# Attention's gate and output blocks all ahead of z, and the last four blocks of the other gate moved in front of the delta rule's output projection

## The chip, the cores and the metric
The kernel runs on one NeuronCore of one Trainium2 chip. The metric is the device time of one execution in microseconds (us), the median of several runs. One program holds instruction streams for five engines: TensorE (PE, matmuls into the eight PSUM banks), VectorE (DVE), ScalarE (ACT), GpSimd (POOL) and SyncE (SP, which issues the DMAs). They meet only through semaphores.

## The reference, cut to what matters
Two transformer blocks in float32 on x of 256 tokens by 2048 features. The change is in the first block's mixer, which adds latent attention and a gated delta rule, each through its own output matrix and its own gate:

```
h = rmsnorm(x) * (1 + sc_a) + sh_a
p = h @ w_in                 # c_q, c_kv, k_pe, q_g, k_g, v_g, z, b, a, gate_logits
y_a = mla_branch(...) @ w_o_mla                   # attention
o   = gated_delta_chunked(q, k, v, beta, g)       # 8 heads of 128
o   = o * rsqrt(mean(o * o) + eps) * gdn_norm * silu(z)
y_b = o @ w_o_gdn
g_a, g_b = split(sigmoid(gate_logits))
x = x + gt_a * ((g_a * y_a + g_b * y_b) @ w_o)
```

Feed-forward layers and the whole second block follow and are not touched.

## The kernel before, in words
Activations lie feature-major, as [128 features, 256 tokens] for each of 16 slices. Each float32 value is kept as a high part and a low part in a reduced format, side by side: H1 holds h so (16 slices of 512 columns), H2 the inputs of the other projections. Weights come as 128x128 tiles, eight to a unit of 512 KB, in exactly the order in which the program uses them. For each unit ACT makes the high part (`hi`, L566, into HI), DVE the low part (`lo`, L722, into LO), and PE multiplies, adding hi·hi, hi·lo and lo·hi. A "wide" tile does this with two matmuls, one of 512 and one of 256 columns (L360 to L364), a narrow one with three of 256 (L366 to L368). There are five buffers for raw units (`NRAW`) and three each for HI and LO. Between the units of this region the same five buffers also take rows of the ada matrix, three for four units, which DVE reduces with one instruction each (`unit_dot`, L710). SP issues every load, in the order of the program, each when its buffer is free.

The order of all work is written by one Python walk, `walk`, that every engine's program replays. `block` emits the tiles of one output and hands its evacuation over with `later(generator, lag)`; `w.flush()`, called each second tile, takes one step of each pending generator that is due, usually three or four tiles (`LAG`, `EVLAG`) after its last step. `need(list, i)` looks at whether a result has been emitted; if not, `force()` takes a step of pending generators whether they are due or not. This orders instructions and is no wait on the chip by itself.

The stages around the change, with their tiles:
- the attention heads, pipelined beside the delta rule (`gdn`, a pending generator whose steps lie four tiles apart). Attention's eight outputs are split into H2[8..15].
- `gate_b(j)`, j from 0 to 15: a wide block of 16 tiles, H1 times w_in; its result is half of a sigmoid (sum, then tanh) in GB[j] (in the trace GBT). GB shares its memory with H2[0..7].
- `gate_a(j)`: a wide block of 16 tiles for YA[j], then a narrow block of 8 tiles over H2[8..15] with w_o_mla, attention's output; `ev_ya` multiplies it with the gate on DVE (L768).
- z: eight wide blocks of 16 tiles; sum, tanh and one multiplication each. Z lies in B1, over the delta rule's k and v of heads 0 to 3, so `need(hg_done, 0)` stands ahead of it.
- `onorm` and `gated(h)`: the delta rule's output is normed, multiplied with Z[h] (L764) and split by ACT (L577) and DVE (L760) into H2[8 + h], where attention's output was. For this `gated` does nothing until `mo_read[0]` is set: the count of the tile that reads attention's outputs last.
- the delta rule's projection w_o_gdn, narrow, 128 tiles over H2[8..15]: the first five outputs interleaved, then eleven one by one. `ev_yb` multiplies with GB[j] (L768), adds YA[j] (L764) and splits into H1[j] (L577, L758); this needs `h1_free`, the last tile that reads H1 for the gates. In its course x is loaded once more (`reload`, L323, four loads of 512 KB, due 24 tiles into the stage, waiting for `x_free`).
- w_o, 256 tiles, and the rest of the network.

Of the kernel before, what the change touches and what calls it, by code (L numbers as in the profile page):

```python
# [85 lines left out]
class Walk:  # L86
# [25 lines left out]
    def now(self):  # L112
        return [(s, n) for s, n in self.count.items() if s in SIGNALS]

    def later(self, gen, lag=0, gap=LAG):
        self.pending.append([self.tile + lag, gen, gap])
# [22 lines left out]
    def need(self, lst, i):  # L139
        while lst[i] is None:  # L140
            self.force()
        return lst[i]
# [26 lines left out]
def run(gen):  # L169
    for _ in gen:  # L170
        pass
# [30 lines left out]
def program(nc, xT, pos, cols_d, consts_d, wada, wst, bias_d, gain_d, out, log):  # L202
# [8 lines left out]
    with ctx:  # L211
# [96 lines left out]
        def sync(e):  # L308
# [35 lines left out]
            def store(m, a, ready):  # L344
                q.wait_ge(ready)
                e.dma_start(out[:, m, a:a + 1024], YT[:, m, a:a + 1024]).then_inc(S["out"], 16)

            walk(dict(load_cols=load_cols, load_consts=load_consts, load_x=load_x, load_x2=load_x2, load_pos=load_pos,
                      load_ada=load_ada, load_unit=load_unit, load_bias=load_bias, load_gain=load_gain, store=store), log)
            e.wait_ge(S["out"], 16 * N_STORES)  # L350

        def tensor(e):
# [184 lines left out]
            def conv_square_sum(bk, a, square, free):  # L537
                q.wait_ge(square, free)
                for j in range(a, a + 4):
                    r = e.matmul(bk[:, 0:256], cn("ones"), B1[:, j, :], start=(j == 0), stop=(j == 7))  # L540
                r.then_inc(S["cv_p"], 1)

            walk(dict(tile=tile, tile_tokens=tile_tokens, x_turn=x_turn, direct=direct, c_spread=c_spread, spin=spin, stat_add=stat_add, stat_sum=stat_sum, acc2_sum=acc2_sum, rope_turn=rope_turn, kpe_swap=kpe_swap, ba_turn=ba_turn,
                      cumulate=cumulate, row_sum=row_sum, spread=spread, g_spread=g_spread, g_heads=g_heads, g_turn=g_turn,
                      g_turn_mt=g_turn_mt, g_pair=g_pair, g_ws=g_ws, g_state=g_state, g_out=g_out, turn=turn,
# [3 lines left out]
        def scalar(e):  # L549
# [131 lines left out]
            def conv_tanh(y, t, ready, free):  # L681
                q.wait_ge(ready, free)
                e.activation(y, t, ACT.Tanh, scale=0.5).then_inc(S["cv_a"], 1)

            walk(dict(c_sigmoid=c_sigmoid, half_row=half_row, modulated=modulated, hi=hi, copy_sum=copy_sum, split_hi=split_hi, tanh=tanh, sigmoid=sigmoid, square=square,
                      gained=gained, square_sum=square_sum, root_table=root_table, root_guess=root_guess, sine=sine, beta=beta, softplus=softplus, gate_exp=gate_exp, row_square=row_square,
                      soft_exp=soft_exp, soft_scale=soft_scale, tap_first=tap_first, conv_first=conv_first, padded=padded, turned_rows=turned_rows, turned=turned, g_exp=g_exp, g_copy=g_copy, conv_square=conv_square, conv_affine=conv_affine, conv_tanh=conv_tanh))
# [297 lines left out]
        def walk(mine, log=None):  # L985
            w = Walk(mine)
# [135 lines left out]
            def block(H, toks, k0, wname, kbase, n, evac, order=None, wide=False):  # L1122
                return blocks(H, toks, k0, wname, kbase, [(n, evac)], order, wide)
# [348 lines left out]
            def l2norm(hg):  # L1472
                order = [(b + 4 * hg + i, n + i) for i in range(4) for b, n in ((8, 4), (0, 0))]
                while None in [qkv_tok[j] for j, n in order]:
                    yield
                bi, bk, fr = mbank.get()
                for c, (j, n) in enumerate(order):
                    i, t, ft = te.get()
                    a = do("row_square", "l2_a", t, B1[:, j, :], qkv_tok[j], ft)
                    yield  # L1480
                    m = do("row_sum", "l2_p", bk, n, t, c == 0, c == 7, a, fr)
                    te.release(i, m)
                yield
                need(H2_tok, 7)
                while rs_busy[0]:
                    yield
                rs_busy[0] = True
                r = yield from rsqrt_steps(RS[:, 0, :], RS[:, 1, :], bk[:, 0:256], 1.0, 1e-6, m, H2_tok[7], rs_used[0])
                mbank.release(bi, r)
                yield  # L1490
                for n in range(0, 8, 2):
                    bi, bk, fr = mbank.get()
                    m = do("spread", "l2_p", bk, n, r, fr)
                    rs_used[0] = m
                    yield
                    for i in range(2):
                        j = (0 if n < 4 else 8) + 4 * hg + n % 4 + i
                        qkv_tok[j] = do("unit_rows", "l2_v", bk, j, i, 128.0 ** -0.5 if n < 4 else 1.0, m)
                    mbank.release(bi, qkv_tok[j])
                l2_tok[hg] = qkv_tok[j]  # L1500
                rs_busy[0] = False
# [369 lines left out]
            mo_read = [None]  # L1871
# [14 lines left out]
            def ev_gate(dst, toks, j, free):  # L1886
                def f(bk, tok, own):
                    k = yield from raw_sum(dst[j], bk, tok, own, free)
                    yield
                    toks[j] = do("tanh", "ev_a", dst[j], dst[j], 0.5, k)  # L1890
                return f

            def ev_ya(j):
                def f(bk, tok, own):
                    ya_tok[j] = do("scaled", "ev_v", YA[j], YA[j], 1.0, bk[:, 0:256], add, mult, tok, need(ga_tok, j))
                    own[0].release(own[1], ya_tok[j])
                    yield
                return f

            def gate_a(j):  # L1900
                run(block(H1, h_tok, 0, "w_in", 0, 42 + j, ev_gate(YA, ga_tok, j, mla_free), wide=True))
                run(block(H2, mo_tok, 8, "w_o_mla", 0, j, ev_ya(j)))

            def gate_b(j):
                run(block(H1, h_tok, 0, "w_in", 0, 58 + j, ev_gate(GB, gb_tok, j, up_free), wide=True))
# [2 lines left out]
                ups(h)  # L1908
            up_free = ("tile", w.tile)
            later(l2norm(1), 0, 6)  # L1910
            for j in range(16):
                gate_b(j)
            need(mo_tok, 7)
            mla_free = now()
            for j in range(12):
                gate_a(j)
            need(hg_done, 0)
            for j in range(8):
                run(block(H1, h_tok, 0, "w_in", 0, 33 + j, ev_z(j), wide=True))
            for j in range(12, 16):  # L1920
                gate_a(j)
            h1_free = mo_read[0] = ("tile", w.tile)
            need(hg_done, 1)
            x_free = now()

# [633 lines left out]
```

## Time and profile before

| | us |
|---|---|
| median of 3 runs | 2774.64 (2770.35 to 2775.34) |
| the profiled execution's own time | 2774.21 |
| its span, first to last instruction | 2772.4 |
| mean granted TensorE clock | 0.992 |
| PE busy | 2697.3 (97%) |
| DVE busy | 1943.1 (70%) |
| ACT busy | 1308.3 (47%) |

Times in rows are microseconds from the start of the span, durations of single instructions nanoseconds where it says so. Consecutive matmuls overlap, so a matmul's own duration is longer than the distance to the next one; PE's pace is read from the starts. "idle before <-releaser" is how long the engine stood idle before an instruction and what ended that. The clock is a share of 2.4 GHz.

### The profile page before, as it was taken

Reading aid. Unit: us, or ns where it says so; the run is one execution under the profiler, and the core shown is the slowest. Engines: PE = TensorE matmul, PEld = TensorE weight load, DVE = VectorE, ACT = ScalarE, POOL = GpSimd, SP = SyncE. Lnnn points to the kernel's source line nnn. Section 1 sums busy time; section 2 is a strip of 40 time slices with the busy share of each in tenths; the row PEclk is TensorE's granted clock in tenths of the full one; section 3 lists DMA queues with packets and bytes.
Section 4 is the critical chain, followed back from the end, with each engine's and each line's share of the span. In section 5 each row is a group of like instructions: output and inputs, shape, how many; then the busy total and the mean of one; then the engine's idle time right before and its main releaser. Section 6 shows DMA issues by size and latency. Waiting matters only on the chain.

```text
span 2772.4 us, 41156 instructions
## 1 busy us (share of the span) xinstructions
PE 2697.3 (97%) x16208; PEld 2391.9 (86%) x16208; DVE 1943.1 (70%) x2998; ACT 1308.3 (47%) x2047; POOL 142.9 (5%) x132
## 2 busy tenths in 40 slices
PE   8989999999999999999999999999999999999998
PEld 7778988988899888888888889998888888888887
DVE  6768777777896886556555679997667466575665
ACT  2165544334444554444444454457554444443443
POOL 0000000000002000000000170111100000000000
PEclk9999999999999999999999999999999999999999
DMA  9944245667986786555555555544545555555554
GB/s 386 401 143 154 100 153 185 218 212 271 312 299 235 249 301 208 190 190 186 188 189 190 188 176 168 180 167 136 172 154 177 194 190 193 193 186 195 190 191 144
DMA packets 158161, 565.19 MB, mean 204 GB/s; under 512 B 17552, under 2 KB 21904, under 8 KB 157840
## 3 DMA queue, kind: packets, MB, share of 16 engines
q1 hardware_dynamic: 157968, 562.56, 59.4%
q8 instruction: 128, 2.10, 0.3%
q14 instruction: 65, 0.53, 0.1%
HBM read 560.39 MB, written 2.10 MB: 203 GB/s over the span
## 4 chain that ended last, share of the span: by engine, by line
PE 83%; DVE 9%; DMA 3%; ACT 3%; issue 1%; SPq 0%; DVEq 0%; POOL 0%; ACTq 0%
PE BK L363 17%; PE BK L361 17%; PE BK L364 9%; PE BK L360 8%; PE BK L377 4%; PE BK L375 4%; PE BK L376 4%; PE BK L366 4%; PE BK L368 4%; PE BK L367 4%; DVE LO L722 3%; PE BK L473 2%; DVE B L934 2%; DMA EARLY<-wst_dram 2%; PE BK L388 1%
## 5 line engine op out<-in xcount | busy, mean ns | idle before, releaser
L566 ACT ACTIVATE HI<-RAW 128x1024 fp32r<-128x1024 f32 x824 | 873.3, 1060 | 1182.7 <-PE BK L361 635.8
L722 DVE TENSOR_TENSOR LO<-RAW,HI 128x1024 fp32r<-128x1024 f32 x824 | 1013.0, 1230 | 387.1 <-ACT HI L566 386.0
L363 PE MATMUL BK<-H,HI 128*128 128x512 f32 x2160 | 869.3, 405 | 17.3 <-DVE LO L722 16.8
L361 PE MATMUL BK<-H,HI 128*128 128x512 f32 x2128 | 841.2, 397 | 0.0
L364 PE MATMUL BK<-H,LO 128*128 128x256 f32 x2160 | 602.0, 279 | 0.0
L360 PE MATMUL BK<-H,LO 128*128 128x256 f32 x2128 | 596.0, 280 | 0.2 <-DVE H L760 0.2
L360 PEld LDWEIGHTS BK<-H,LO 128*128 128x128 f32 x2128 | 401.6, 189 | 93.8 <-DVE H L760 0.6
L364 PEld LDWEIGHTS BK<-H,LO 128*128 128x128 f32 x2160 | 408.7, 189 | 85.1 <-issue 0.7
L363 PEld LDWEIGHTS BK<-H,HI 128*128 128x128 f32 x2160 | 412.1, 191 | 29.9 <-DVE LO L722 21.0
L361 PEld LDWEIGHTS BK<-H,HI 128*128 128x128 f32 x2128 | 401.0, 188 | 3.8
L366 PE MATMUL BK<-H,HI 128*128 128x256 f32 x1280 | 377.1, 295 | 14.3 <-DVE LO L722 7.9
L368 PE MATMUL BK<-H,LO 128*128 128x256 f32 x1280 | 363.7, 284 | 0.0
L367 PE MATMUL BK<-H,HI 128*128 128x256 f32 x1280 | 363.7, 284 | 0.0
L366 PEld LDWEIGHTS BK<-H,HI 128*128 128x128 f32 x1280 | 247.0, 193 | 19.4 <-DVE LO L722 11.5
L367 PEld LDWEIGHTS BK<-H,HI 128*128 128x128 f32 x1280 | 247.0, 193 | 1.5
L368 PEld LDWEIGHTS BK<-H,LO 128*128 128x128 f32 x1280 | 246.7, 193 | 0.0
L375 PE MATMUL BK<-HI,H 128*128 128x512 f32 x512 | 199.2, 389 | 0.0
L377 PE MATMUL BK<-HI,H 128*128 128x512 f32 x512 | 199.2, 389 | 0.0
L376 PE MATMUL BK<-LO,H 128*128 128x512 f32 x512 | 199.2, 389 | 0.0
L760 DVE TENSOR_TENSOR H<-TV,H 128x256 fp32r<-128x256 f32 x116 | 49.0, 425 | 167.5 <-ACT H L577 167.3
L376 PEld LDWEIGHTS BK<-LO,H 128*128 128x128 f32 x512 | 96.1, 188 | 20.2
L377 PEld LDWEIGHTS BK<-HI,H 128*128 128x128 f32 x512 | 96.1, 188 | 20.1
(268 smaller groups left out, 2554.1 us busy)
## 6 DMA issues: line engine op xcount, KB each, us to landing
RAW<-wst_dram SPq DMA_DIRECT2D x838, 512.0 KB, 3.4
RAW<-wada_dram SPq DMA_DIRECT2D x154, 512.0 KB, 4.8
EARLY<-wada_dram SPq DMA_DIRECT2D x38, 512.0 KB, 12.4
EARLY<-wst_dram SPq DMA_DIRECT2D x18, 512.0 KB, 13.8
X<-xT_dram SPq DMA_DIRECT2D x8, 512.0 KB, 7.3
B<-bias_dram SPq DMA_DIRECT2D x32, 128.0 KB, 3.3
out_dram<-B SPq DMA_DIRECT2D x4, 512.0 KB, 2.7
B<-gain_dram SPq DMA_DIRECT2D x1, 1024.0 KB, 4.6
```

What stands on the lines that cost most here:

```text
L360: e.matmul(bk[:, 256:512], ll, H[:, k, 0:256], start=False, stop=False, skip_group_check=True)
L361: e.matmul(bk[:, :], hh, H[:, k, :], start=False, stop=last, skip_group_check=True).then_inc(S["tile"], 1)
L363: e.matmul(bk[:, :], hh, H[:, k, :], start=first, stop=False, skip_group_check=True)
L364: e.matmul(bk[:, 256:512], ll, H[:, k, 0:256], start=False, stop=last, skip_group_check=True).then_inc(S["tile"], 1)
L366: e.matmul(bk[:, 0:256], hh, H[:, k, 0:256], start=first, stop=False, skip_group_check=True)
L367: e.matmul(bk[:, 0:256], hh, H[:, k, 256:512], start=False, stop=False, skip_group_check=True)
L368: e.matmul(bk[:, 0:256], ll, H[:, k, 0:256], start=False, stop=last, skip_group_check=True).then_inc(S["tile"], 1)
L375: e.matmul(bks[m][:, :], H[:, k, 128 * m:128 * m + 128], hh, start=first, stop=False, skip_group_check=True)
L376: e.matmul(bks[m][:, :], H[:, k, 128 * m:128 * m + 128], ll, start=False, stop=False, skip_group_check=True)
L377: r = e.matmul(bks[m][:, :], H[:, k, 256 + 128 * m:384 + 128 * m], hh, start=False, stop=last, skip_group_check=True)
L566: e.activation(HI[:, u % NHL, :], raw_at(slot), ACT.Copy).then_inc(S["hi"], 1)
L722: e.tensor_tensor(LO[:, u % NHL, :], raw_at(slot), HI[:, u % NHL, :].bitcast(f32), sub).then_inc(S["lo"], 1)
```

## The change
Twelve of the 16 gate b blocks stay in front; then come all 16 pairs of gate a and attention's output, behind which `mo_read` is set; then z; then the last four gate b blocks, behind which `h1_free` is set. The number and the form of the tiles stay the same, and no new function is called.

```
             later(l2norm(1), 0, 6)
-            for j in range(16):
+            for j in range(12):
                 gate_b(j)
             need(mo_tok, 7)
             mla_free = now()
-            for j in range(12):
+            for j in range(16):
                 gate_a(j)
+            mo_read[0] = ("tile", w.tile)
             need(hg_done, 0)
             for j in range(8):
                 run(block(H1, h_tok, 0, "w_in", 0, 33 + j, ev_z(j), wide=True))
             for j in range(12, 16):
-                gate_a(j)
-            h1_free = mo_read[0] = ("tile", w.tile)
+                gate_b(j)
+            h1_free = ("tile", w.tile)
             need(hg_done, 1)
             x_free = now()
```

## Rows read from the trace of the kernel before

**Rows 1.** The page: busy time; GB/s in 40 slices of 69 us
```profile
PE 2697.3 (97%) x16208; PEld 2391.9 (86%) x16208; DVE 1943.1 (70%) x2998; ACT 1308.3 (47%) x2047; POOL 142.9 (5%) x132
...
GB/s 386 401 143 154 100 153 185 218 212 271 312 299 235 249 301 208 190 190 186 188 189 190 188 176 168 180 167 136 172 154 177 194 190 193 193 186 195 190 191 144
```
**Rows 2.** What PE waited for, 380 to 860 us: total, times, longest
```profile
PE BK L366 <- DVE H L760: 5.3, 1, 5.3
...
PE BK L445 <- DVE RS L780: 0.3, 1, 0.3
```
**Rows 3.** PE in order of time: start, duration, engine, line, operation, operands
```profile
744.16 0.28 PE L367 MATMUL BK<-H,HI 128*128 128x256 f32 x1
744.28 0.28 PE L368 MATMUL BK<-H,LO 128*128 128x256 f32 x1
749.89 0.56 PE L366 MATMUL BK<-H,HI 128*128 128x256 f32 x1 [5.33 <-DVE H L760]
...
755.15 0.41 PE L366 MATMUL BK<-H,HI 128*128 128x256 f32 x1
...
758.38 0.28 PE L366 MATMUL BK<-H,HI 128*128 128x256 f32 x1
...
761.26 0.28 PE L366 MATMUL BK<-H,HI 128*128 128x256 f32 x1
```
**Rows 4.** Stretches: length, PE, PEld, DVE, ACT, POOL busy, clock, DMA share, GB/s
```profile
744.00:750.00 6.00, 0.67 (x6) 0.50 (x4) 6.00 (x16) 4.67 (x12) 0.00 (x0) 0.93 0.98 337
750.00:756.00 6.00, 6.00 (x29) 6.00 (x30) 4.43 (x10) 0.55 (x1) 0.00 (x0) 0.50 0.97 324
...
767.00:804.60 37.60, 35.96 (x290) 34.88 (x289) 37.50 (x73) 17.64 (x26) 0.00 (x0) 1.00 0.82 274
```
**Rows 5.** DVE in order of time around the boundary
```profile
746.31 2.76 DVE L764 TENSOR_TENSOR B<-B 128x256 f32<-128x256 f32 x8
...
749.32 2.77 DVE L760 TENSOR_TENSOR H<-B,H 128x256 fp32r<-128x256 f32 x8
```
**Rows 6.** ACT in order of time around the boundary
```profile
747.11 2.55 ACT L577 ACTIVATE H<-B 128x256 fp32r<-128x256 f32 x8
755.45 1.06 ACT L566 ACTIVATE HI<-RAW 128x1024 fp32r<-128x1024 f32 x1 [5.79 <-PE BK L368]
```
**Rows 7.** Line 445, the spread of norms, 645 to 700 us: durations, first and last start
```profile
L445 PE MATMUL BK<-RS,CN x8: 377/379/482, 654.2 to 657.2; 128*128 128x256 f32 x8
```
**Rows 8.** Line 760, attention's last splits: durations, first and last start
```profile
L760 DVE TENSOR_TENSOR H<-BK,H x2: 415/420/425, 373.7 to 381.4; 128x256 fp32r<-128x256 f32 x2
```
**Rows 9.** The stretch of z, columns as in rows 4
```profile
663.80:708.40 44.60, 44.60 (x258) 38.92 (x257) 39.96 (x58) 21.43 (x31) 0.00 (x0) 1.00 0.93 336
```
**Rows 10.** Low halves on DVE, and the first matmuls of their units
```profile
701.40 1.23 DVE L722 TENSOR_TENSOR LO<-RAW,HI 128x1024 fp32r<-128x1024 f32 x1
705.62 0.39 PE L363 MATMUL BK<-H,HI 128*128 128x512 f32 x1
762.62 1.23 DVE L722 TENSOR_TENSOR LO<-RAW,HI 128x1024 fp32r<-128x1024 f32 x1 [0.45 <-ACT HI L566]
767.02 0.28 PE L366 MATMUL BK<-H,HI 128*128 128x256 f32 x1
775.39 1.22 DVE L722 TENSOR_TENSOR LO<-RAW,HI 128x1024 fp32r<-128x1024 f32 x1
776.66 0.39 PE L366 MATMUL BK<-H,HI 128*128 128x256 f32 x1 [0.84 <-DVE LO L722]
```
**Rows 11.** The loads of x: issue on SP, and issue to landing; weights' landing, 745 to 815
```profile
748.06 1.76 SPq L323 DMA_DIRECT2D X<-xT_dram  x4
...
DMA to landing us min/median/max: 5.6/7.3/9.5
...
DMA to landing us min/median/max: 3.4/4.7/6.9
```

More of the change, by code:

```diff
@@ L1910, in walk @@
             later(l2norm(1), 0, 6)
-            for j in range(16):
+            for j in range(12):
                 gate_b(j)
@@ L1914, in walk @@
             mla_free = now()
-            for j in range(12):
+            for j in range(16):
                 gate_a(j)
+            mo_read[0] = ("tile", w.tile)
             need(hg_done, 0)
@@ L1920, in walk @@
             for j in range(12, 16):
-                gate_a(j)
-            h1_free = mo_read[0] = ("tile", w.tile)
+                gate_b(j)
+            h1_free = ("tile", w.tile)
             need(hg_done, 1)
```

## The prediction
> **What bounds the kernel now.** First the profile's page [rows 1]: TensorE (PE) is busy 97% of the span, and the table above gives a mean clock of 0.992. Time can be won only where PE stands still or is slow. The list of what PE waited for, from 380 to 860 us, then has one large entry: a single wait of 5.3 us on a split of a delta-rule output (DVE, L760); its eight other entries are 6.4 us together [rows 2]. That wait is where the change is, so the rest is read around it.
>
> PE's order of time: the last matmul of the last gate a pair (attention's output projection) starts at 744.28, the first one of the delta rule's projection at 749.89 [rows 3]. At the pace just before (one matmul in 0.12 us) it was due at 744.40, so 5.49 us are lost. The reader is to see what follows too: the next unit (eight tiles) takes from 749.89 to 755.15, 5.26 us, the one after it 3.23 us, the one after that 2.88 us [rows 3]. From 750 to 756 the granted clock is 0.50, that is 1.2 GHz in place of 2.4; it had been full in z [rows 9] and is full from 767 on [rows 4]. The slow clock costs (5.26 - 2.88) + (3.23 - 2.88) = 2.73 us.
>
> Why PE waited: the code lets the eight gated outputs overwrite attention's outputs in H2 only behind `mo_read`, which is set behind the last gate a pair. So all eight multiplications (L764, 2.76 us), all eight high halves on ScalarE (ACT, 2.55 us) and the low halves (L760) stand in one bunch behind 744.4, and from 744 to 750 DVE has no free time at all [rows 4 to 6]. The inputs were there long before: the spread of the norms for the second four heads was over at 657 us [rows 7].
>
> **What is removed.** With all 16 gate a pairs in front of z, `mo_read` is set 192 tiles earlier in tile order (z's 128 and the last 64 of gate b), and each gated output waits only for its own z. By tiles, z starts 32 tiles later than before: four more pairs (96 tiles) less four gate b blocks (64). The last z output then needs some 13 tiles of its own (lags of 4, 3, 3 and 3 tiles), and a gated output three more steps; about 64 - 25 tiles remain before the projection, at 2.79 us for eight (z's 16 units in 44.6 us [rows 9]) some 13 us. So the eight splits are ready and the wait goes, 5.49 us, and with PE at work there is no reason for the half clock, 2.73 us: **8.2 us** together.
>
> **What is moved.** PE's tiles are the same in number and form, 640 wide ones and 128 narrow ones; where they stand does not change their cost. Everything up to the twelfth gate b block is unchanged. Attention's outputs, which gate a now wants 64 tiles earlier, were split by 381.4 + 0.4 us [rows 8], when gate b had only begun; no wait there. Loads go by units of eight tiles and not by stage, so weights and ada rows keep their order against the tiles. The sums of gate b 12 to 15 and their tanh lie where those of gate a 12 to 15 lay, less four multiplications of DVE; nothing at the boundary waits for them, since gate b is read output by output.
>
> **What the gated work costs in its new place.** It is no longer beside an idle PE. In z's stretch, 663.8 to 708.4, DVE is busy 40.0 of 44.6 us while PE has no gap [rows 9]. Eight pairs of operations cost 2.76 + 2.77 = 5.5 us [rows 5]; some six of the eight fall in z, 4.1 us against 4.6 free, the other two in gate b, where DVE has one sum for 16 tiles in place of z's two operations. DVE would be near full for 30 us. What protects PE is the lead: the low half (LO, L722) of the unit that starts on PE at 705.62 was ready at 702.63 (1.23 us from 701.40), 3.0 us early [rows 10]. A lead of 2 to 3 us takes bunches of one or two operations. Bounds: nothing, and 5.5 us, if each operation held PE for its whole time. I take 0.6 us, near nothing: DVE still has a little more free time than work to take, and the work comes one output at a time. ACT, busy 21.4 of the 44.6, takes its eight (2.55 us) at no cost.
>
> **What the reload costs.** A thing that the diff does not name: the four loads of x (512 KB each) are due 24 tiles into the projection, but a wait in the program's order (`need` on the first gated output) forces everything pending, so before they were issued at 748.06, inside the stall [rows 11]. With the outputs ready nothing is forced, and they go out three units later, among the weights of a PE at full pace. They landed 5.6 to 9.5 us after issue, weights in 4.7 at the median [rows 11]. The DMA engines are busy 0.93 of z's time at 336 GB/s [rows 9], and the fastest slice of the kernel moved 401 GB/s [rows 1]; four loads are 2.1 MB, 5.2 us at that rate. Weights behind them come up to 5.2 us late. Two things hide it: the lead of about 3.2 us that the projection builds up once PE sets the pace (low half ready at 762.62 + 1.23 = 763.85, its unit on PE at 767.02 [rows 10]), and that the late weights are used from unit eight of the stage on, where DVE is the limit anyway: from 767 on it is busy 37.5 of 37.6 us [rows 4], and PE waits for it, 0.84 us at 776.66 [rows 10]. Bounds: nothing, and 5.2 us. I take 0.8, nearer to nothing, because DVE's own queue there is longer than the delay. The same limit stays in the second part of the projection whatever comes before; I count no change for it, as the five-output bunch starts at the same tile.
>
> The Trainium skill ("DMA: Bandwidth & Descriptors", section "Bandwidth") speaks against the change here: it puts the limit from HBM at about 358 GB/s for one core when both of a pair stream. By that figure the 2.1 MB would take an estimated 5.9 us and the reload's term would be 1.5 in place of 0.8. This trace disagrees for this core: 401 GB/s over a slice of 69 us [rows 1].
>
> **Sum.** -8.2 + 0.6 + 0.8 = -6.8 us. The profiled execution took 2774.21 us (span 2772.4, 1.8 around it), 0.4 below the median of 2774.64; it should go to 2767.4, and the median to **2767.8 us**. What can be told from no change is 0.2%, 5.5 us, so the forecast is only just beyond it.
>
> **The rivals.**
> *A smaller win, 2770 to 2774.* The wait goes, but DVE or the late weights take part back in small gaps: with half of each upper bound, 2.75 us in z (the lead used up as at 776.66, where LO was ready at 776.61 and PE waited [rows 10]) and 2.6 us at the reload, 8.2 - 5.35 = 2.9 us remain: 2771.8. For it: DVE at 90% and DMA at 93%, both to be raised [rows 9]. Against: at those shares PE had no gap. Chance 0.22.
>
> *The change doesn't do what it says, 2774.6.* The last outputs are late still, and PE waits as long for them. The last gated output would have to be split 5.5 us behind the last tile of gate b; by the count above it is some 13 us ahead of it. Chance 0.05.
>
> *Slower, 2780.9.* The four loads of x stop PE. If a weight issued right behind them lands as late as the longest of them, 9.5 us, and its high half (1.06 us) and low half (1.23 us) come on top with nothing of it hidden, PE stands still 11.8 us in one piece. Its clock then falls once more (2.73 us), and 14.5 - 8.2 = 6.3 us are lost net. It decides from a wait of 5.5 us on (8.2 - 2.73). For it: five weight buffers only, DMA already at 0.98 around the boundary [rows 4]. Against: that weight is not wanted at once, the lead of 3.2 us must be eaten first, and DVE's queue is in front of it. Chance 0.05.
>
> *The forecast*, 5 to 8.2 us won: chance 0.68.
>
> **How the numbers follow.** Beyond 0.2% (5.5 us) lies most of the forecast's own range: 0.58. Within 0.2%: the rest of it (0.10), the smaller win (0.22), no effect (0.05) and, of the slower case, the 0.01 in which only a part of the 11.8 us shows: 0.38. Slower: 0.04. The range reaches down to the full 8.2 us and the half of the 5 us by which the three runs differ, 2763.9, and up through the smaller win to 2773.0. The forecast's own range is 2766.4 to 2769.7.
>
> **What would show it.** Right: no wait of PE for L760 in this region; eight L764 `B<-B` spread over 40 us, not in one row; the clock at 1.0 across the boundary; X's loads some three units behind the projection's first matmul; z and gate b units still 2.79 us. Wrong: waits of PE for LO L722 in z's last blocks (DVE term), or in units 8 to 11 of the projection with HI waiting for `wst_dram` (reload term), above all one long enough to halve the clock. If the win is whole but the median shows less, a stage further on gave it back; I see none, since PE paces all of it.

## The result, and the profile after

The changed kernel takes 2777.62 us (median of 20 runs, 2773.74 to 2782.08), the kernel before 2772.79 us (20 runs on the same chip, 2770.35 to 2776.16): a ratio of 1.0015, 95% interval 1.0009 to 1.0021. It is 4.8 us slower by the medians (4.2 by the ratio), and the interval does not reach 1; that is inside the 0.2% that the prediction set as its bound and on the other side of zero from its forecast of 2767.8. The profiled execution has a span of 2775.7 us, 3.3 more than before.

The page after, busy times and DMA rate, against [rows 1]:

```profile
PE 2694.3 (97%) x16208; PEld 2389.2 (86%) x16208; DVE 1942.7 (70%) x2998; ACT 1307.7 (47%) x2047; POOL 143.3 (5%) x132
GB/s 386 401 144 154 98 160 186 219 204 248 307 318 242 232 297 220 191 188 189 187 188 189 190 170 172 184 164 140 167 157 178 196 190 190 193 187 196 190 190 144
```

The work is the same. What PE waited for from 380 to 860 us, largest groups (sum us, count, longest one), against [rows 2]:

```profile
PE BK L366 <- DVE LO L722: 7.6, 3, 4.5
PE BK L363 <- DVE LO L722: 4.4, 6, 1.5
PE BK L467 <- DVE X L904: 1.9, 1, 1.9
PE BK L473 <- ACT B L671: 1.5, 5, 0.3
```

The one wait of 5.3 us on `DVE H L760` is gone, and waits for LO (L722), the low half of a unit of weights, have come. PE's timeline at a few places, against [rows 3]:

```profile
655.00 0.38 PE L366 MATMUL BK<-H,HI 128*128 128x256 f32 x1 [2.79 <-DVE LO L722]
...
751.60 0.40 PE L361 MATMUL BK<-H,HI 128*128 128x512 f32 x1
751.83 0.28 PE L366 MATMUL BK<-H,HI 128*128 128x256 f32 x1
...
774.73 0.28 PE L368 MATMUL BK<-H,LO 128*128 128x256 f32 x1
...
779.47 0.58 PE L366 MATMUL BK<-H,HI 128*128 128x256 f32 x1 [4.46 <-DVE LO L722]
```

The boundary at 751.83 has no gap, as forecast. But a gap of 4.46 us stands 28 us behind it and one of 2.79 us 97 us ahead of it. To see where the time went, the place of fixed units on PE is read from both timelines. A unit is eight tiles, and the same unit number has the same number of tiles ahead of it in either order. Their form is not quite the same: a narrow unit takes 2.88 us and a wide one 2.79, and by that the stretch from 145 to 152 is 0.2 us longer in the new order and the one from 152 to 176 0.4 us shorter. Worked out from the starts of units 115, 145, 152 (where z begins in the new order) and 176 (the delta rule's projection), and the end of unit 226's low half on DVE:

| stretch on PE, us | before | after | difference |
|---|---|---|---|
| beside the delta rule's end (115 to 145) | 127.91 | 131.92 | +4.0 |
| to the new start of z (145 to 152) | 22.01 | 23.33 | +1.3 |
| z and the blocks up to the boundary (152 to 176), without the wait of 5.49 | 69.43 | 73.50 | +4.1 |
| the wait itself | 5.49 | 0 | -5.5 |
| the projection and what follows (176 to 226) | 156.37 | 157.74 | +1.4 |
| together | 381.21 | 386.49 | +5.3 |

The sum agrees with the 4.8 us of the medians. The last stretch holds two terms: the half clock that is gone (the first three units of the projection take 8.62 us, 11.37 before, so -2.7) and something new of about +4.1. So 8.2 us were won as forecast, and 13.5 lost in four places. Single profiles shift by some 1.6 us at units 80 to 84 (26.93 us before, 25.35 after), ahead of all this and whatever the kernel; so stretches are compared here, not ends. How far one stretch varies by itself is seen where kernels below have the same code up to its end: 131.35 to 132.52 us for 115 to 145 and 23.05 to 23.60 for 145 to 152 (four profiles in the new order), 72.54 to 73.52 for 152 to 176 (three).

Each place by its windows. The columns are length, PE, PEld, DVE, ACT, POOL, granted clock, DMA share and GB/s; z with the last gate b is the first:

```profile
678.33:751.83 73.50, 70.16 (x402) 60.20 (x401) 62.77 (x98) 35.97 (x58) 0.00 (x0) 1.00 0.88 303
...
655.00:660.00 5.00, 5.00 (x23) 4.45 (x24) 3.90 (x7) 0.00 (x0) 0.00 (x0) 0.66 0.83 262
...
771.00:775.00 4.00, 4.00 (x34) 3.81 (x32) 2.45 (x6) 0.00 (x0) 0.00 (x0) 1.00 1.01 409
775.00:779.00 4.00, 0.01 (x1) 0.00 (x0) 2.10 (x3) 1.36 (x2) 0.00 (x0) 0.91 0.95 369
779.00:785.00 6.00, 5.53 (x26) 5.53 (x27) 6.00 (x12) 2.73 (x4) 0.00 (x0) 0.50 0.82 266
```

**In z** no single gap stands out: PE is busy 70.2 of 73.5 us, its four waits for LO add to 3.3 us, and the gated work is spread as forecast, its last split done 10.9 us ahead of the boundary (two groups of those on the tiles B and H between 679 and 752):

```profile
L764 DVE TENSOR_TENSOR B<-B x8: 424/426/427, 692.6 to 736.3; 128x256 f32<-128x256 f32 x8
L760 DVE TENSOR_TENSOR H<-B,H x8: 413/420/428, 695.5 to 740.5; 128x256 fp32r<-128x256 f32 x8
```

ACT's waits in the same stretch are long: its high halves stand behind weight loads. That is not new with the change: it waits 29.3 us for them in the 80.6 us from 663.8 to 744.4 of the kernel before, where PE waits for nothing. What is new in the stretch is the gated work on DVE.

```profile
ACT HI L566 <- DMA RAW<-wst_dram: 31.9, 16, 3.3
```

**In the projection** the chain behind the gap of 4.46 us runs over several engines. SP's queue, then ACT's and DVE's timelines:

```profile
762.77 1.80 SPq L323 DMA_DIRECT2D X<-xT_dram  x4
```
```profile
777.11 1.06 ACT L566 ACTIVATE HI<-RAW 128x1024 fp32r<-128x1024 f32 x1 [8.07 <-DMA RAW<-wst_dram]
```
```profile
775.82 1.28 DVE L710 CUSTOM_DVE_ANT_0 RAW<-RAW,ADA,MOD 128x1024 f32<-128x1024 f32 x1 [2.36 <-DMA RAW<-wada_dram]
778.19 1.23 DVE L722 TENSOR_TENSOR LO<-RAW,HI 128x1024 fp32r<-128x1024 f32 x1 [1.08 <-ACT HI L566]
```

The four loads of x go out 11 us behind the boundary. They and the weights then move 409 GB/s, just above the 401 of the page's fastest slice; an ada row and a weight come late, ACT and DVE start late, PE stands still from 775 to 779, and its clock is 0.50 for the six us behind. The place is unit eight of the stage, with HI waiting for `wst_dram`: the prediction's own sign that its reload term is wrong. Landing times there (min, median, max): the four loads of x first, then the weights between 752 and 800:

```profile
DMA to landing us min/median/max: 6.1/7.8/10.4
DMA to landing us min/median/max: 3.6/4.8/10.6
```

What the change took away here is a reserve of weights. Behind the stall of the kernel before, ACT waits for PE to give buffers back, so the raw weights have landed already; behind the boundary of the changed kernel it waits for the loads themselves. Before first, then after:

```profile
758.64 1.06 ACT L566 ACTIVATE HI<-RAW 128x1024 fp32r<-128x1024 f32 x1 [2.14 <-PE BK L368]
761.52 1.06 ACT L566 ACTIVATE HI<-RAW 128x1024 fp32r<-128x1024 f32 x1 [1.82 <-PE BK L368]
```
```profile
758.96 1.06 ACT L566 ACTIVATE HI<-RAW 128x1024 fp32r<-128x1024 f32 x1 [2.18 <-DMA RAW<-wst_dram]
761.64 1.06 ACT L566 ACTIVATE HI<-RAW 128x1024 fp32r<-128x1024 f32 x1 [1.62 <-DMA RAW<-wst_dram]
```

**At the delta rule's end**, which the prediction passed over, ACT's timeline shows the output norm (RS, L604 to L606) between a weight and the gate's tanh (B, L581):

```profile
646.71 1.06 ACT L566 ACTIVATE HI<-RAW 128x1024 fp32r<-128x1024 f32 x1 [2.08 <-PE BK L368]
647.79 1.28 ACT L600 ACT_TABLE_LOAD   x1
649.09 0.47 ACT L604 ACTIVATE RS<-BK,CO 128x256 f32<-128x256 f32 x1
649.59 0.42 ACT L606 ACTIVATE RS<-RS 128x256 f32<-128x256 f32 x1
650.03 1.28 ACT L581 ACT_TABLE_LOAD   x1
651.33 0.42 ACT L581 ACTIVATE B<-B 128x256 f32<-128x256 f32 x1
```
```profile
645.23 0.42 DVE L726 TENSOR_TENSOR B<-BK,TE 128x256 f32<-128x256 f32 x1
651.85 0.42 DVE L768 SCALAR_TENSOR_TENSOR B<-B,BK 128x256 f32<-128x256 f32 x1 [6.20 <-PE BK L364]
653.73 1.22 DVE L722 TENSOR_TENSOR LO<-RAW,HI 128x1024 fp32r<-128x1024 f32 x1
```

The sum of gate a (L726) is done at 645.65. Its tanh waits on ACT behind the norm and two table loads of 1.28 us, until 651.33. DVE runs its work in order, so it stands 6.20 us at the multiplication L768 (the releaser named, PE, was done long before; the tanh ends at 651.75 and L768 starts at 651.85). The low half at 653.73 is queued behind it: its high half was done at 647.77 (646.71 + 1.06), and it comes 6 us later. That is PE's 2.79 us at 655.00. Before, a gate a pair ran here as well, but at another phase against the norm: with its pairs (24 tiles each) starting 64 tiles earlier, the pair that meets the norm is in another of its steps. Before's own rows at the place, DVE and ACT, show the product done before the norm's table load:

```profile
645.38 0.42 DVE L768 SCALAR_TENSOR_TENSOR B<-B,BK 128x256 f32<-128x256 f32 x1 [2.83 <-PE BK L361]
```
```profile
648.34 1.28 ACT L600 ACT_TABLE_LOAD   x1
```

### The profile page after: what moved, and what is told of

Its sections match the earlier page's. It is cut to its first block, busy times and chain, and to the rows that moved or that the text cites. A ratio compares the mean times of both kernels' runs of the same rounds, so it can differ in the third digit from the quotient of the medians.

```text
span 2775.7 us, 41144 instructions
## 1 busy us (share of the span) xinstructions
PE 2694.3 (97%) x16208; PEld 2389.2 (86%) x16208; DVE 1942.7 (70%) x2998; ACT 1307.7 (47%) x2047; POOL 143.3 (5%) x132
## 4 chain that ended last, share of the span: by engine, by line
PE 85%; DVE 6%; DMA 4%; ACT 3%; issue 1%; SPq 0%; POOL 0%; DVEq 0%; ACTq 0%
PE BK L363 17%; PE BK L361 16%; PE BK L364 8%; PE BK L360 8%; PE BK L366 5%; PE BK L368 5%; PE BK L367 5%; PE BK L375 4%; PE BK L376 4%; PE BK L377 4%; PE BK L473 2%; DVE LO L722 2%; DMA RAW<-wst_dram 1%; DMA EARLY<-wst_dram 1%; ACT HI L566 1%
## 5 line engine op out<-in xcount | busy, mean ns | idle before, releaser
L722 DVE TENSOR_TENSOR LO<-RAW,HI 128x1024 fp32r<-128x1024 f32 x824 | 1013.0, 1230 | 382.4 <-ACT HI L566 381.5
L363 PEld LDWEIGHTS BK<-H,HI 128*128 128x128 f32 x2160 | 411.0, 190 | 37.5 <-DVE LO L722 28.8
L760 DVE TENSOR_TENSOR H<-TV,H 128x256 fp32r<-128x256 f32 x116 | 49.0, 425 | 170.2 <-ACT H L577 170.0
L377 PEld LDWEIGHTS BK<-HI,H 128*128 128x128 f32 x512 | 96.1, 188 | 20.2
L375 PEld LDWEIGHTS BK<-HI,H 128*128 128x128 f32 x512 | 96.1, 188 | 20.0
```

The lines of the kernel that those rows point to most:

```text
L363: e.matmul(bk[:, :], hh, H[:, k, :], start=first, stop=False, skip_group_check=True)
L375: e.matmul(bks[m][:, :], H[:, k, 128 * m:128 * m + 128], hh, start=first, stop=False, skip_group_check=True)
L377: r = e.matmul(bks[m][:, :], H[:, k, 256 + 128 * m:384 + 128 * m], hh, start=False, stop=last, skip_group_check=True)
L722: e.tensor_tensor(LO[:, u % NHL, :], raw_at(slot), HI[:, u % NHL, :].bitcast(f32), sub).then_inc(S["lo"], 1)
```

## The experiments

Each kernel had 11 timed runs beside 21 or 33 of the kernel before, whose medians were 2774.19 (first four kernels below), 2773.13 (next four), 2774.47 (next four) and 2773.27 (last two). Those whose name ends in b are controls: the same edit in the kernel before, without the change. Stretches are those of the table above; each is from one profile. The diffs are cut to their changed lines, with `...` where a line is cut.

| kernel | edit to | median us (range) | ratio to before (95%) |
|---|---|---|---|
| reload_apart | after | 2777.51 (2773.52-2779.63) | 1.0013 (1.0004-1.0022) |
| reload_late | before | 2777.07 (2772.34-2778.93) | 1.0006 (0.9997-1.0015) |
| gated_late | after | 2776.74 (2773.75-2780.39) | 1.0013 (1.0004-1.0022) |
| z_last | after | 2775.43 (2772.72-2777.5) | 1.0005 (0.9996-1.0014) |
| onorm_8 | after | 2770.99 (2768.16-2773.58) | 0.9991 (0.9982-1.0) |
| ada_front | after | 2776.13 (2773.25-2780.42) | 1.0011 (1.0002-1.0019) |
| ada_front_b | before | 2771.11 (2766.61-2775.15) | 0.9993 (0.9984-1.0002) |
| reload_small | after | 2776.34 (2771.39-2778.43) | 1.0008 (0.9999-1.0017) |
| onorm_8b | before | 2773.68 (2772.21-2775.9) | 0.9998 (0.9989-1.0007) |
| both | after | 2771.21 (2768.95-2773.28) | 0.9989 (0.998-0.9998) |
| both_b | before | 2772.59 (2771.17-2776.96) | 0.9993 (0.9985-1.0002) |
| both_mid | after | 2768.29 (2767.17-2772.7) | 0.9981 (0.9972-0.999) |
| both_mid_b | before | 2771.47 (2767.53-2773.28) | 0.9989 (0.998-0.9998) |
| mid_no_norm | after | 2773.53 (2767.67-2777.69) | 0.9999 (0.999-1.0008) |

**reload_apart.** Is it the bunch of four loads, or their bytes?

```diff
-                yield
+                    yield
...
-            later(reload(), 24)
+            later(reload(), 8, 28)
```

> The changed kernel with the four loads of x issued one by one, 8, 36, 64 and 92 tiles into the delta rule's projection, instead of all four at 24; only SP's order differs. Theory: the four loads in a row are what stops PE for 4.5 us at 775 and then halves its clock for some 6 us. Apart, that wait goes, and of the 4.8 us by which the changed kernel is slower than the one before some 3.6 us come back: about 1.2 us slower than before, 2774. Rival: DVE limits this stage in any case and only hides behind the loads; then the time stays within 1 us of the changed kernel, 4 to 5 us slower than before.

The `yield` now stands inside the loop, so the loads go out one by one. Ratio 1.0013 against 1.0015: no gain, as the rival said. The projection's stretch is 157.20 us against 157.74, and the gap of 4.46 us became five gaps of 4.0 us together. Spreading does not help; whether it is the bytes, reload_small tests.

```profile
PE BK L366 <- DVE LO L722: 4.0, 5, 1.6
```

**reload_late.** The reverse, in the kernel before: the loads of x no longer leave inside the stall.

```diff
-            later(reload(), 24)
+            later(reload(), 24, 8)
```

(`force` passes over generators whose steps lie further apart than `LAG`, so a step of 8 keeps the loads to their due place.)

> The kernel before, with its block order untouched, but its four loads of x kept to their due place, 24 tiles into the projection (they are no longer drawn forward by the forced step). Theory: the late loads cost here what they cost in the changed kernel, 3 to 4 us more than before, with a wait of PE for a low half in the second half of the projection. Rival: the wait of 5.3 us at the boundary has filled the weight buffers, so that the loads find more room here and cost less than 1 us.

The loads go out at 762.1 to 763.5. The wait at the boundary stays and a second one comes 28 us behind it, at the place where the changed kernel has its own:

```profile
750.03 0.55 PE L366 MATMUL BK<-H,HI 128*128 128x256 f32 x1 [6.13 <-DVE H L760]
...
777.79 0.39 PE L366 MATMUL BK<-H,HI 128*128 128x256 f32 x1 [2.33 <-DVE LO L722]
```

So x outside the stall stops PE in the old order of blocks too; the gap is half of the changed kernel's 4.46 us, with ACT waiting for PE and not for weights until 767. The time is inconclusive: 1.0006 with no change inside the interval.

**gated_late.** Z in its new place, but the gated outputs again in one bunch at the boundary.

```diff
-            mo_read[0] = ("tile", w.tile)
...
-            h1_free = ("tile", w.tile)
+            h1_free = mo_read[0] = ("tile", w.tile)
```

> The changed order of blocks, but the eight gated outputs held back to the projection as before, so that the wait at the boundary is there again and the loads of x are issued inside it. Theory: what is left is the cost of the new order beside the delta rule's end, 1.3 us in the middle and 3.8 us at its end, so about 5 us slower than before; and z and gate b run at 2.79 us per unit because the gated work is not among them. Rival: z is slow for another reason than the gated work (smaller lead from the delta rule's end, the ada row's change of half inside z); then z's units still wait for low halves and the kernel is 8 to 10 us slower than before.

The wait of the boundary is back, and z runs free: 68.64 us from 680.26 to 748.90 without a wait, against 73.50.

```profile
PE BK L366 <- DVE H L760: 4.7, 1, 4.7
```
```profile
680.26:748.90 68.64, 68.64 (x402) 60.06 (x400) 57.42 (x83) 32.72 (x49) 0.00 (x0) 1.00 0.91 326
```

So the gated work among z's tiles costs 4 to 5 us of PE, about as much as the wait that it takes away. In this stretch ACT still waits 27.6 us for weights (31.9 with the gated work), and PE has no gap. Behind the wait the clock is at 0.50 again and the first three units take 11.42 us (8.62 in the changed kernel). The loads of x go out inside the wait (751.9 to 753.2), and PE has no long gap in the projection, whose stretch is that of before (156.4). The ratio of 1.0013 is that of the changed kernel within noise, and the theory's 5 us slower (1.0018) lies in its interval.

**z_last.** All 16 gate b blocks ahead of z, so that nothing lies between z and the projection; the loads of x as in reload_apart.

```diff
-            for j in range(12):
+            for j in range(16):
                 gate_b(j)
...
-            for j in range(12, 16):
-                gate_b(j)
...
-                yield
+                    yield
...
-            later(reload(), 24)
+            later(reload(), 8, 28)
```

> All 16 gate b blocks first, all 16 gate a pairs, then z and at once the projection, with the loads of x one by one as in reload_apart. The order is that of the kernel before up to the end of the delta rule. Theory: no cost beside the delta rule (the 5 us of the changed kernel are absent); at the boundary only the last z output is late, a wait of 2 to 3 us without a fall of the clock in place of 5.5 + 2.7; so 3 to 5 us faster than before. Rival: the chain behind the last z output is as long as the bunch was, PE waits 5 us again and the time is that of before.

Ratio 1.0005 (0.9996 to 1.0014): the forecast of 3 to 5 us faster failed. One part of the theory held: with gate a's pairs where they were before, the stretches beside the delta rule are those of before (127.91 and 22.10 us). But z costs 2.9 us and the projection, with the wait and the loads of x in it, 3.4 us more than before. The wait for the last gated output is 3.1 us; it stands at 763.98, 17 us into the projection, whose first matmul at 747.25 has no gap, and the clock is at 0.76 for the six us behind it. There are small waits for LO as well (5.2 us in nine). So the last four gate b blocks are worth that wait, and are not what costs the time.

```profile
PE BK L366 <- DVE H L760: 3.1, 1, 3.1
PE BK L366 <- DVE LO L722: 2.7, 6, 0.9
PE BK L363 <- DVE LO L722: 2.5, 3, 1.3
```

**onorm_8.** The output norm of each half of the delta rule's heads, the second one eight tiles later. Nothing else is changed.

```diff
-                    later(onorm(hg))
+                    later(onorm(hg), 8 * hg)
```

> The changed kernel with the norm of the second four heads started eight tiles later, so that ACT does a gate's tanh ahead of the norm's table load and not between its two table loads. Theory: the wait of 2.8 us at the end of the delta rule and the half clock behind it come from DVE standing 6.2 us at attention's gate multiplication, whose tanh is stuck on ACT behind the norm; with the tanh ahead they go, and 3 to 4 us of the changed kernel's loss come back by unit 148: about 1 us slower than before. Rival: the loss only moves, since the later stages are short of DMA and DVE time; then less than 1 us is left of it at the end and the time is 4 to 5 us slower than before.

The tanh comes first now, the two table loads behind it, DVE stands 2.77 us in place of 6.20, and PE has no gap there. The stretch 115 to 145 is 128.54 us (131.92 without the edit, 127.91 before), and the ratio falls from 1.0015 to 0.9991: 0.0024 of 2773, 6.7 us, with intervals that do not touch. By the stretches it is 6.3 us up to unit 226, 4.8 of them between 115 and 152 and 1.8 in z (71.73 in place of 73.50). The theory had the mechanism and put its worth at 3 to 4 us.

```profile
646.53 0.40 ACT L581 ACTIVATE B<-B 128x256 f32<-128x256 f32 x1
...
650.00 1.28 ACT L600 ACT_TABLE_LOAD   x1
```
```profile
647.04 0.42 DVE L768 SCALAR_TENSOR_TENSOR B<-B,BK 128x256 f32<-128x256 f32 x1 [2.77 <-PE BK L361]
```

**ada_front.** Eight of the ada rows, each of them a load and an instruction on DVE (L710), due earlier, so that fewer fall into z and the projection.

```diff
-... 64 + (i - 80) * 3 // 4 if i < 208 ...
+... 64 + (i - 80) * 7 // 8 if i < 144 else 120 + (i - 144) * 5 // 8 if i < 208 ...
```

> The changed kernel with eight of the ada rows (a load of 512 KB and a reduction of 1.28 us on DVE each) moved from units 144 to 208, where z and the projection lie, forward to units 80 to 144, beside the delta rule. Theory: z and the projection of the changed kernel are limited by DVE and by the loads at once; with a sixth less of both their low halves come early again, and 4 to 6 us come back: 0 to 1 us slower than before or faster. Rival: beside the delta rule the rows cost as much as they save; then the change against the changed kernel is under 1 us.

**ada_front_b** is the same edit to the kernel before.

> The same move of eight ada rows in the kernel before. Theory: there the wait at the boundary stays (it is a bunch of operations and not a shortage) and z has no wait to lose, so within 1.5 us of before; the difference to the gain in the changed kernel is what the change has made scarce. Rival: the rows are a burden for both in the same way, and both kernels gain the same.

In ada_front z takes 68.69 us (73.50) with the gated work inside and without a wait of PE, and ACT's waits for weights are 9.2 us (31.9); the projection is 153.53 us (157.74). But the stretch 115 to 145 rises from 131.92 to 135.04, and some 2.3 us are lost in units 80 to 112. The rows mostly moved their cost. The ratio is 1.0011, about 1 us below the changed kernel's 1.0015 and not to be told from it, near the rival. In the control the wait at the boundary is 3.4 us with the clock at full behind it; its ratio is 0.9993, with no change inside the interval.

```profile
686.45:755.14 68.69, 68.69 (x403) 60.17 (x402) 58.49 (x91) 36.09 (x57) 0.00 (x0) 1.00 0.87 297
```

**reload_small.** A quarter of the bytes of x. The other 12 slices of x keep old data, so this kernel is for timing alone.

```diff
-e.dma_start(X[:, 4 * i:4 * i + 4, :], xT[:, 4 * i:4 * i + 4, :])
+e.dma_start(X[:, i:i + 1, :], xT[:, i:i + 1, :])
```

> The changed kernel with each of the four loads of x cut to a quarter (one slice of 256 columns of its four; the other 12 slices of x are not loaded again, so the residual is formed from old data there). Theory: the 2.1 MB are what delays the weights; with 0.5 MB the wait of 4.5 us and the half clock behind it go, and 3 to 4 us come back: about 1 us slower than before. Rival: the weights are late in the projection even without x, as z left no lead; then a wait for low halves remains there and less than 1 us comes back.

The projection's stretch is 153.85 us against 157.74, and PE's waits for LO there fall to 1.3 us in three. The clock stays at full there. By this stretch the reload's price is 3.9 us. By the runs it is 1.0008 against 1.0015, some 2 us in the forecast direction, with intervals that overlap.

```profile
PE BK L366 <- DVE LO L722: 1.3, 3, 0.9
```

**onorm_8b** is the control of onorm_8 in the kernel before.

> The kernel before with the norm of the second four heads started eight tiles later, as in onorm_8. There its table loads do not stand between a gate's sum and its tanh. Theory: nothing to win, within 1.5 us of before; then the 7 us by which onorm_8 beat the changed kernel belong to the change's own collision with the norm. Rival: the shift helps every order of blocks, and this kernel too is 3 us or more faster than before.

Ratio 0.9998 (0.9989 to 1.0007). The delay of the norm is worth nothing there that can be told from noise, so the 6.7 us are particular to the new order and not a general saving.

**both** joins onorm_8 and ada_front; **both_b** is its control.

> The changed kernel with the norm eight tiles later (onorm_8) and eight ada rows moved forward (ada_front). Theory: the three losses are separate places: no wait at the end of the delta rule, z at 2.79 us per unit, no wait of 4 us or more in the projection, and the boundary without a wait; the rows' 3 us beside the delta rule stay. 3 to 6 us faster than before. Rival: they overlap, and it is no better than onorm_8 alone (2 us faster).

> The kernel before with both shifts of the run called both. Theory: the wait at the boundary and the half clock behind it remain, so it is 2 us faster than before as with the rows alone, and slower than both by 2 to 4 us, which is what the change of order is worth once its three costs are out of the way. Rival: the order is worth nothing even then, and both_b equals both.

0.9989 against 0.9993, 1.1 us apart where 2 to 4 were expected, and not to be told apart; nor are the two together more than the norm alone gives (0.9991). The rows again take time beside the delta rule (134.25 us).

**both_mid** and its control **both_mid_b**: the norm's delay, and rows left alone until unit 112, then brought forward faster.

```diff
-... 64 + (i - 80) * 3 // 4 if i < 208 ...
+... 64 + (i - 80) * 3 // 4 if i < 112 else 88 + (i - 112) if i < 144 else 120 + (i - 144) * 5 // 8 if i < 208 ...
```

> As both, but the eight ada rows are added in units 112 to 144 and not from 80 on, so that units 80 to 112, where the first part of the delta rule is, keep theirs. Theory: the rows moved cost less there (DVE is 74% busy between 530 and 640), so 1 to 2 us better than both. Rival: they fall on the norm's table loads or the last steps of the delta rule, and it is 1 us or more worse than both.

> The kernel before with the two shifts of both_mid (norm eight tiles later, eight ada rows added in units 112 to 144). Theory: the order of blocks is worth 2 to 4 us once its costs are out of the way, so this control is 1 to 3 us faster than before, against 5 to 6 us for both_mid. Rival: the win of both_mid is that of the rows and the norm alone; then this kernel is 5 us faster too.

both_mid is the fastest kernel measured here, 0.9981, 5 us below the kernel before and 9 below the changed one (0.0019 and 0.0034 of 2773). Its stretches are 133.00, 21.96, 68.68 and 154.45 us, 378.09 together against 381.21 before and 386.49 after, and the list of PE's waits from 640 to 870 us has three groups left.

```profile
PE BK L366 <- DVE LO L722: 2.1, 1, 2.1
PE BK L440 <- ACT TE L631: 1.4, 2, 0.9
PE BK L445 <- DVE RS L780: 0.2, 1, 0.2
```

The control is at 0.9989, with a wait of 3.4 us left at the boundary and the clock at full behind it. The order itself may be worth 2 us once its collisions are out; the intervals overlap, so this is not shown. Nor is it shown that both_mid beats both (0.9989).

**mid_no_norm** has both_mid's rows and not the norm's delay.

> The changed kernel with the eight ada rows in units 112 to 144 and the norm where it was. Theory: the collision of the norm's table loads with the gate's tanh comes back and costs the 5 us that it cost in the changed kernel; z and the projection are as in both_mid: 0 to 1 us faster than before. Rival: the rows and the norm overlap (with the rows moved, the collision falls elsewhere), and it is as fast as both_mid.

0.9999 against both_mid's 0.9981: about 5 us for the collision with the norm, also with the rows moved. The stretches say the same and say where: 136.11 and 24.28 us against 133.00 and 21.96 from 115 to 152, 5.4 us, with one wait of PE for LO of 5.1 us.

## Why the prediction was wrong

**The bound and the stall: right.** The wait on L760 is gone, the clock is 1.0 over the boundary, the gated work is spread over 48 us. The term of 8.2 us stands: gated_late brings a wait of 4.7 us and 2.8 us of slow clock back by moving `mo_read` alone.

**"What is moved": "where they stand does not change their cost", a term of nothing: the step that failed.** Up to the twelfth gate b block nothing changed, as the prediction said, and up to unit 115 the stretches agree but for the shift at 80 to 84. The cost comes behind that. The prediction treated the moved tiles by number and form, and did not ask what small work of other chains they meet. Gate a's pairs start 64 tiles earlier and meet the delta rule's norm in another step; their tanh and the norm share ACT, their product and the weights' low halves share DVE's queue. The stretches 115 to 152 cost 5.3 us. onorm_8, which only starts this norm later, gives 6.7 us back by the runs and 4.8 by the two stretches (131.92 + 23.33 less 128.54 + 21.96), its control nothing; mid_no_norm against both_mid finds 5 us once more, and z_last, which leaves gate a's pairs in place, has no cost there. This one term is as large as the whole loss, and no rival of the prediction had it.

**"What the gated work costs", 0.6: the size was off.** It measured 4.1 us by the table and 4.9 against gated_late, near the upper bound of 5.5; 3.1 are left in onorm_8 (71.73 less 68.64), so up to 1.8 us of it are the norm's meeting, carried on into z. The sign "z and gate b units still 2.79 us" failed: 73.50 us for 24 units are 3.06. The argument of free time was taken from DVE alone, and the stretch shows a second shortage: ACT waits 31.9 us for weights, so high halves, and behind them low halves, have little lead. Either alone is borne: gated_late has nearly the same waits of ACT (27.6 us) without the gated work, and ada_front has the gated work with waits of 9.2 us, and both take 68.7 us without a gap. That DVE could not use its free moments because they lay behind late inputs is argued from this and not shown. Rows take both DVE and DMA, so which of the two ran short first stays open.

**"What the reload costs", 0.8: the size was off.** It measured 3.9 us (reload_small) to 4.1 (the table). The forced issue and the new place, some three units in, were read rightly, and the slower rival had the mechanism, a late weight that stops PE and halves its clock; it was given 0.05 and a gap of 11.8 us, where the gap is 4.46. That the time came out slower is thus no win for that rival: at the measured size its term alone would have left the change a win. What failed is "DVE's own queue there is longer than the delay": DVE stood still as well, 2.36 us for an ada row, since the rows that it works on are loads themselves, late by the same bytes; reload_small has no such wait. The prediction had used the 37.5 of 37.6 us in [rows 4] as slack that hides a delay. That figure begins where the first five outputs are evacuated (766.64 in the kernel before). Ahead of it DVE had no backlog: between 754 and 766 it waited four times for a high half, 5.0 us together. What the kernel before had in reserve were landed weights, behind the stall; the changed kernel had none.

The Trainium skill ("DMA: Bandwidth & Descriptors", section "Bandwidth") gives about 358 GB/s for each core when both cores of a pair stream; by it the term would have been an estimated 1.5. This program runs on one core, so the 401 GB/s that the prediction set against the page, and the 409 GB/s over 4 us here, do not contradict it: the page speaks of another case. Neither rate gives the size. The bytes alone are 5.2 us at the prediction's 401 GB/s, and 3.9 of them reached PE.

**The sum** that the runs make is -8.2 + 4.1 + 4.1 + 5.3 = +5.3, beside 4.8 measured. With the two sized terms corrected and the meeting with the norm left out it would be 0.0, no change. onorm_8 measures that case: 1.0 us faster than before by its stretches, 2.5 by the runs with no change at the edge of the interval. So the two sizes alone would have cost the forecast most of its 6.8 us, and what tips it to slower is the term that was not there. The terms are not quite apart, as the 1.8 us in z show.

What is only argued: that the old stall itself paid for x and for the gated work. It fits the rows (x left at 748.06 in the stall and no wait followed; ACT behind the stall waited for PE and not for weights; reload_late takes x out of the stall and a wait of 2.33 us appears; gated_late puts it back and the wait is gone), but reload_late's time does not settle it.

## What to carry over

A stall on the bounding engine can be time in which other queues catch up, as the weight loads did here; before counting it as won, list the loads and vector work that ran in it, and price each at its new place with the slack of all engines on its chain, not of one. When blocks move, look up what small chains (norms, table switches, gates) run at the old and at the new tiles, on every in-order engine, even where the blocks are alike in number and form. In the changed kernel a delay of eight tiles for one norm gave back more than the reordering had lost, and in the kernel before it gave nothing: such a meeting belongs to one order of work, and has to be looked for in each.

## What the hardware showed that was not expected

- On ACT, one norm between two tanh cost two table loads of 1.28 us around 0.9 us of work; the chain from it (tanh late, DVE standing 6.20 us, low half late, PE standing 2.79 us) carried it over three engines.
- PE's clock was granted at 0.50 (1.2 GHz) for the six us behind a gap of 4.46 us, and at 0.66 on average over the five us behind one of 2.79 us; over the boundary without a gap it stayed at full. Gaps of equal length did not always cost the same: behind a boundary wait of 3.4 us the clock was 1.00 over six us in ada_front_b and both_mid_b, and 0.72 in both_b.
- One core drew 409 GB/s over 4 us with its DMA engines at their full share; weights around it took up to 10.6 us to land, against a median of 4.8.
